# Raising the variances of every norm to the power -0.5 on GpSimd, in a hybrid decoder stack kernel

## The reference, cut to what matters

```python
def layer_norm(x, g, b):                # 3 per layer of the first stack, 6 in all
    mu = mean(x); var = mean(square(x - mu))
    return (x - mu) * rsqrt(var + 1e-5) * g + b
def rms_norm(x, g):                     # latents of the attention; all norms of the second stack
    return x * rsqrt(mean(square(x)) + 1e-6) * g
...
for l in range(2):                      # first stack
    h = layer_norm(ALPHA * h + 0.5 * swiglu(h, up1, down1), ...)
    h = layer_norm(ALPHA * h + hybrid_mixer(h, ...), ...)
    h = layer_norm(ALPHA * h + 0.5 * swiglu(h, up2, down2), ...)
for l in range(2):                      # second stack
    h = h + token_mixing(rms_norm(h), ...)
    h = h + (swiglu_2 if l == 0 else moe_swiglu)(rms_norm(h), ...)
out = rms_norm(h)
```

## Time and profile before

| | |
|---|---|
| median of 3 runs | 2813.24 us (2811.03, 2813.24, 2813.75) |
| profiled execution, span from first to last instruction | 2809.8 us (no other time of this execution is given) |
| PE busy | 2745.6 us, 98% of the span |
| DVE busy | 1982.1 us, 71% |
| ACT busy | 1608.7 us, 57% |
| POOL busy | 700.7 us, 25% |
| HBM | 661.01 MB read, 236 GB/s over the span |

### The profile page before, as it was taken

One profiled execution on the slowest core, in us unless ns is written; L12 is line 12 of the kernel. 1 busy time (PEld: TensorE's weight loads), 2 busy tenths in 40 slices (PEclk: granted clock), 3 DMA queues, 4 the chain that ended last, 5 costly groups with the idle time before them and its releaser, 6 DMA issues.

```text
span 2809.8 us, 68032 instructions
## 1 busy us (share of the span) xinstructions
PE 2745.6 (98%) x28028; PEld 2292.6 (82%) x28028; DVE 1982.1 (71%) x1914; ACT 1608.7 (57%) x1723; POOL 700.7 (25%) x562
## 2 busy tenths in 40 slices
PE   9999999999999999999999999999999999999997
PEld 7887788888877888887888887888879788797794
DVE  5457575564576755666855566778899898998986
ACT  5445663354356554455643445657677776777765
POOL 4314022122122221120122011144234243242331
PEclk9999999999999999999999999999999999999999
DMA  9764367576643676553576663469999999999995
GB/s 240 171 199 124 91 194 195 169 191 176 188 134 106 180 206 178 157 181 121 179 189 180 200 187 124 151 240 365 383 386 383 387 387 378 394 383 382 388 384 223
DMA packets 657516, 665.64 MB, mean 237 GB/s; under 512 B 25302, under 2 KB 513116, under 8 KB 657276
## 3 DMA queue, kind: packets, MB, share of 16 engines
q1 hardware_dynamic: 655696, 659.75, 71.5%
q0 software_dynamic: 704, 0.59, 0.4%
q10 hardware_dynamic: 876, 1.79, 0.2%
HBM read 661.01 MB, written 1.05 MB: 236 GB/s over the span
## 4 chain that ended last, share of the span: by engine, by line
PE 91%; DVE 4%; ACT 2%; issue 1%; DVEq 1%; DMA 0%; POOLq 0%; ACTq 0%; SPq 0%; POOL 0%
PE ps L2084 23%; PE ps L2085 23%; PE ps L2086 23%; PE ps L2814 3%; PE ps L2813 3%; PE ps L2812 3%; PE ps L2127 1%; PE ps L2133 1%; PE ps L2128 1%; DVE w_lo L1258 1%; PE ps L2437 1%; PE ps L2417 1%; ACT w_hi L705 1%; PE ps L2747 1%; PE ps L2505 1%
## 5 line engine op out<-in xcount | busy, mean ns | idle before, releaser
L2084 PE MATMUL ps<-x_hi,w_hi 128*128 128x128 f16 (+2 forms) x5440 | 1229.5, 250 | 16.1 <-DVE prod L1273 5.4
L2085 PE MATMUL ps<-x_lo,w_hi 128*128 128x128 f16 (+2 forms) x5440 | 1229.2, 250 | 0.0
L2086 PE MATMUL ps<-x_hi,w_lo 128*128 128x128 f16 (+2 forms) x5440 | 1229.0, 250 | 0.0
L1258 DVE SCALAR_TENSOR_TENSOR w_lo<-w,w_hi 128x2048 f16<-128x2048 f32 (+4 forms) x338 | 692.5, 2059 | 309.4 <-ACT w_hi L705 307.6
L705 ACT ACTIVATE w_hi<-w 128x2048 f16<-128x2048 f32 (+4 forms) x338 | 560.9, 1669 | 83.7 <-PE ps L2086 70.4
L2084 PEld LDWEIGHTS ps<-x_hi,w_hi 128*128 128x128 f16 x5440 | 534.0, 98 | 71.2 <-issue 14.4
L2085 PEld LDWEIGHTS ps<-x_lo,w_hi 128*128 128x128 f16 x5440 | 533.8, 98 | 45.9
L2086 PEld LDWEIGHTS ps<-x_hi,w_lo 128*128 128x128 f16 x5440 | 533.9, 98 | 42.6
L1754 DVE SCALAR_TENSOR_TENSOR w_lo<-w,w_hi 128x2048 f16<-128x2048 f32 x224 | 532.8, 2406 | 40.9 <-ACT w_hi L1178 40.8
L1178 ACT ACTIVATE w_hi<-w 128x2048 f16<-128x2048 f32 x224 | 416.9, 1901 | 28.4 <-DMA w<-in_moe_w_gate 12.0
L2066 POOL CAST ff<-pb 128x512 f16<-128x512 f32 x56 | 137.6, 2458 | 568.5 <-DVE pb L1846 568.5
(11 more groups left out here) (390 smaller groups left out, 4302.3 us busy)
## 6 DMA issues: line engine op xcount, KB each, us to landing
w<-in_ffn_w_up SPq DMA_DIRECT2D x176, 512.0 KB, 5.0
w<-in_moe_w_gate SPq DMA_DIRECT2D x80, 1024.0 KB, 8.1
w<-in_moe_w_up SPq DMA_DIRECT2D x80, 1024.0 KB, 8.7
w<-in_moe_w_down SPq DMA_DIRECT2D x64, 1024.0 KB, 7.8
w<-in_w_in SPq DMA_DIRECT2D x112, 512.0 KB, 4.6
mix<-in_moe_w_down SPq DMA_DIRECT2D x48, 1024.0 KB, 8.0
w<-in_mix_w_in SPq DMA_DIRECT2D x64, 512.0 KB, 4.9
mix<-in_moe_w_gate SPq DMA_DIRECT2D x32, 1024.0 KB, 8.9
```

The costliest lines, as they stand in the source:

```text
L1258: vec.scalar_tensor_tensor(k.w_lo[:, s, 0:size], k.w32[:, s, 0:size], WS, k.w_hi[:, s, 0:size], ALU.mult, ALU.subtract).then_inc(k.parts_r ...
L2084: pe.matmul(acc, w_hi, x_hi, start=first, stop=False)
L2085: pe.matmul(acc, w_hi, x_lo, start=False, stop=False)
L2086: return pe.matmul(acc, w_lo, x_hi, start=False, stop=last)
```

## The change

All roots and reciprocals of norms go. One POOL instruction, a TENSOR_TENSOR with the power as its operation and a column of -0.5 broadcast over the tokens as second operand, takes the place of each pair. DVE brings the variance to SBUF and adds the epsilon there; for the latents and the heads that is a new operation on DVE or ACT. `root_ready` and its table loads go, and at the norms' place ACT's next weight split moves ahead of the last square. The last norm is done per half, so that the first half's scaling can start before the second half's squares are summed.

```diff
+    k.minus_half = sb("minus_half", [P, 1], F32)
...
 (ACT, down_norm; wo_norm, wout_squares and down_squares alike)
                 c = u // 2
                 if c == KC - 1:
-                    root_ready()
+                    split(phase.first + phase.units + AHEAD, quads, UNIT)
                 act.wait_ge(k.vec_evac, vec0 + phase.base + 2 + c + 1)
                 square(n, c)
...
 (ACT, layer_norm)
         act.activation(k.tmp[:, 1, t], k.ps[:, 4, t], ACT.Square).then_inc(k.rest_squared, 1)
-        act.wait_ge(k.ln_spread, n + 1)
-        act.activation(k.std[:, 0, t], k.tmp[:, 1, t], ACT.Sqrt, bias=k.eps[:, 0:1]).then_inc(k.ln_std, 1)
-        split(following + 2, q, UNIT)
...
 (ACT, latents)
-                act.activation(k.sq[:, 0:3, :], k.mix1[:, 12:15, :], ACT.Square).then_inc(k.lat_squared, 1)
-            if u == LAT_ROOT:
-                act.wait_ge(k.lat_mean, l + 1)
-                act.activation(k.std[:, 0, :], k.ps[:, 4, 0:T1], ACT.Sqrt, bias=k.eps[:, 1:2], scale=float(D) / 256)
-                act.activation(k.std[:, 1, :], k.ps[:, 5, 0:T1], ACT.Sqrt, bias=k.eps[:, 1:2], scale=float(D) / 128).then_inc(k.lat_std, 1)
+                act.activation(k.sq[:, 0:2, :], k.mix1[:, 12:14, :], ACT.Square, scale=(D / 256) ** 0.5)
+                act.activation(k.sq[:, 2, :], k.mix1[:, 14, :], ACT.Square, scale=(D / 128) ** 0.5).then_inc(k.lat_squared, 1)
...
 (ACT, take_mean of the mLSTM heads)
-                           ACT.Sqrt, bias=k.eps[:, 2:3], scale=4.0 * float(D) / P).then_inc(k.act_evac, 1)
+                           ACT.Identity, bias=k.eps[:, 2:3], scale=4.0 * float(D) / P).then_inc(k.act_evac, 1)
...
 (DVE, layer_norm)
-        vec.tensor_tensor(k.tmp[:, 1, cols], k.ps[:, 5, cols], k.tmp[:, 1, cols], ALU.subtract).then_inc(k.ln_spread, 1)
+        vec.scalar_tensor_tensor(k.tmp[:, 1, cols], k.ps[:, 5, cols], LN_EPS * WS * WS, k.tmp[:, 1, cols], ALU.add, ALU.subtract).then_inc(k.ln_var_out, 1)
         u(0)
-        vec.wait_ge(k.ln_std, n + 1)
-        vec.reciprocal(k.rstd[:, 0, cols], k.std[:, 0, cols])
         vec.drain()
+        vec.wait_ge(k.ln_rooted, n + 1)
...
 (DVE, rms_norm; the latents alike, over 544 columns)
-        vec.wait_ge(k.rms_std, n + 1)
-        vec.reciprocal(k.rstd[:, 0, 0:T2], k.tmp[:, 0, 0:T2])
-        vec.drain()
+        vec.wait_ge(k.rms_mean, n + 1)
+        vec.tensor_scalar(k.tmp[:, 0, 0:T2], k.ps[:, 5, 0:T2], RMS_EPS, None, ALU.add).then_inc(k.rms_var_out, 1)
+        vec.wait_ge(k.rms_rooted, n + 1)
...
 (DVE, end of the second stack's attention)
         split_gated(12)
-        invert_ml(0)
         split_gated(13)
-        invert_ml(1)
-        vec.drain()
+        vec.wait_ge(k.ml_rooted, 2 * l + 2)
...
 (POOL)
+    def root(out, x, shape):
+        return pool.tensor_tensor(out, x, k.minus_half[:, 0:1].broadcast_to(shape), ALU.pow)
+
+    def ln_root(n):
+        t = kept(n)
+        pool.wait_ge(k.ln_var_out, n + 1)
+        root(k.rstd[:, 0, t], k.tmp[:, 1, t], [P, t.stop - t.start]).then_inc(k.ln_rooted, 1)
...
         down_norm(l * 3)
+        ln_root(l * 3)
+        pool.wait_ge(k.lat_var_out, l + 1)
+        for c in range(2):
+            a = root(k.rstd[:, c, :], k.tmp[:, c, :], [P, T1])
+        a.then_inc(k.lat_rooted, 1)
...
+        for pair in range(2):
+            pool.wait_ge(k.act_evac, s["rest"].base + REST_OUT["mean%d" % pair] + 1 + 2)
+            for h in range(4 + 2 * pair, 6 + 2 * pair):
+                a = root(k.sq[:, h, 0:T2], k.sq[:, h, 0:T2], [P, T2])
+            a.then_inc(k.ml_rooted, 1)
```

More of the change, by code:

```diff
@@ L772, in wo_norm, with layer_norm @@
         square(n, 6)
+        split(phase.first + phase.units + AHEAD, q, UNIT)
         act.wait_ge(k.vec_evac, vec0 + phase.base + 2 + 4)
         square(n, 7)
-    def layer_norm(n, b0, q, following, last=False):
+    def layer_norm(n, b0, last=False):
         act.wait_ge(k.ln_rest, n + 1)
@@ L810, in wout_squares @@
             else:
+                if c == 7 and l == 0:
+                    split(phase.first + phase.units + AHEAD, 0, UNIT)
                 act.wait_ge(k.vec_evac, phase.base + 2 + c // 2 + 1)
@@ L822, in down_squares, with rms_norm @@
         over_units_ahead(act, phase, 0, split, take, loop=False)
[L824 to L830, removed]
+    def rms_norm(n, to_parts=True):
+        if to_parts:
             for c in range(KC):
@@ L892, in act_program @@
         down_norm(l * 3, S1["down1"], q, vec0, take_vectors)
-        layer_norm(l * 3, C1["ln_b"], q, S1["win"].first)
+        layer_norm(l * 3, C1["ln_b"])
         def take_columns(u, b):
@@ L1008, in act_program @@
         wo_norm(l * 3 + 1, l, q, vec0)
[L1009 removed]
+        layer_norm(l * 3 + 1, C1["ln_b"] + KC)
         up(S1["up2"], q, vec0, gates0 + S1["up2"].gates, live(l), b0=C1["ln_b"] + KC)
@@ L1242, in act_program @@
     for b in range(2):
-        act.activation(k.squares[:, b, :], y[:, b, :], ACT.Square, accum_out=k.ms[:, b, 0:1])
-    act.drain()
-    act.activation(k.ms[:, :, 1], k.ms[:, :, 0], ACT.Sqrt, bias=k.eps[:, 1:2], scale=1.0 / D).then_inc(k.final_std, 1)
+        act.activation(k.squares[:, b, :], y[:, b, :], ACT.Square, accum_out=k.ms[:, b, 0:1]).then_inc(k.final_squared, 1)
     for b in range(2):
@@ L1460, in towards_latents @@
             if u == LAT_NORMED:
-                vec.wait_ge(k.lat_std, l + 1)
-                vec.reciprocal(k.rstd[:, :, :], k.std[:, :, :])
-                vec.drain()
+                vec.wait_ge(k.lat_mean, l + 1)
+                vec.tensor_scalar(k.tmp[:, 0:2, :], k.ps[:, 4:6, 0:T1], RMS_EPS, None, ALU.add).then_inc(k.lat_var_out, 1)
+                vec.wait_ge(k.lat_rooted, l + 1)
                 for c in range(3):
@@ L1648, in fox_low @@
                               ALU.subtract).then_inc(k.fox_parts, 1)
-        def invert_ml(pair):
-            vec.wait_ge(k.act_evac, rest.base + REST_OUT["mean%d" % pair] + 1 + 2)
-            for h in range(2 * pair, 2 * pair + 2):
-                vec.reciprocal(k.sq[:, 4 + h, 0:T2], k.sq[:, 4 + h, 0:T2])
         split_gated(2)
@@ L1885, in vec_program @@
     vec.wait_ge(k.final_g_loaded, 16)
-    vec.wait_ge(k.final_std, 1)
-    vec.reciprocal(k.ms[:, :, 2], k.ms[:, :, 1])
-    vec.drain()
     y = k.ps[:, 4:8, :].rearrange("p (b c) n -> p b (c n)", b=2)
     for b in range(2):
+        vec.wait_ge(k.final_squared, b + 1)
+        vec.tensor_scalar(k.ms[:, b, 1:2], k.ms[:, b, 0:1], 1.0 / D, RMS_EPS, ALU.mult, ALU.add).then_inc(k.final_var_out, 1)
+        vec.wait_ge(k.final_rooted, b + 1)
         vec.scalar_tensor_tensor(k.out_rows[:, b, :], y[:, b, :], k.ms[:, b, 2:3], k.final_g, ALU.mult, ALU.mult).then_inc(k.row_ready, 1)
@@ L2077, in pool_program @@
         moe_round(1)
+    for b in range(2):
+        pool.wait_ge(k.final_var_out, b + 1)
+        root(k.ms[:, b, 2:3], k.ms[:, b, 1:2], [P, 1]).then_inc(k.final_rooted, 1)
 def pe_program(pe, k, i, out):
```

39 lines of the change are left out of this document (24 added, 15 removed).

## The result

The changed kernel takes **3690.98 us** (median of 4 runs, 3689.78 to 3692.18) against 2813.49 of the kernel before (4 runs, 2811.03 to 2813.78). The ratio is 1.3116, with a 95% interval of 1.3098 to 1.3135: slower by 31%, or 877 us. The sign of the prediction (slower, with a chance of 0.52) held. Its size (2850) and its range (to 2909) did not.

What follows compares the result with a forecast made beforehand. PE, busy 98% of the span, was taken as the bound, so only its pauses count. Norms, latents and heads less gains lose 27.9 us, the clock 8.5: 36.4 over 2813.2 gives 2850 us, range 2797 to 2909.

Steps and rivals of the forecast that it cites:

- What a power costs on POOL: Step bounding a 272-column power between 3.3 and 7.3 us, using DVE's reciprocal-to-add ratio of 4.3; middle taken, 4.8.
- X: Time of one power of 272 columns on POOL, taken as 4.8 us (4.5 for 256 columns).
- the case above 7.3: Rival of a long function or code fetched on each call: X of 7.3 us and more, 2909 us; chance 0.15.
- layer norms: At the six layer norms the power lengthens the chain from variance to first scaling: 14.5 us lost.
- RMS norms: At the four RMS norms the power lengthens the chain from ACT's root to the first scaling: 10.8 us lost.
- latents: DVE's queue waits behind POOL's powers, so the last low part reaches PE 3.2 us late: 6.4 lost for both layers.
- heads: Four powers a layer end 1.3 us late, within 2 us of slack: no cost; beyond, about 3.8 per microsecond of X.
- less 3.8: Gains in the sum: 2.8 us from table loads at the heads, 1.3 at the last norm, minus 0.3 for latents' squares.
- the clock: PE's longer pauses lower its clock at half of the ten norms: 8.5 us lost, bounds none and 17.
- ACT's loads: 20 table loads go; those ahead of the gate's tanh at the heads win 1.4 us a layer, 2.8 in all.
- the cheap rival: A power is about as cheap as an add (X = 0.77): 15.6 us won, 2797 us; chance 0.33 for X below 2.0.
- Code fetched anew: Part of the rival with X of 7.3 and more: POOL fetches the power's code each time; 2909 us, chance 0.15.

Runs made afterwards that it cites:

- e4: The kernel before, with powers of several shapes, exponents and types added at the end of POOL's program: 2946.5 us.
- e2: The changed kernel with constant products for the powers of latents, RMS norms and heads; the six layer norms and the last norm keep theirs: 3051.6 us.
- e8: The kernel before with per-half last norm, one root for all heads, and ACT's exp(-0.5 ln(x)) for root and reciprocal in the other norms: 2804.2 us.
- e9: The changed kernel with ACT's exp(-0.5 ln(x)) in place of every POOL power but the last norm's; the weight split stays moved: 2800.6 us.
- e1: The changed kernel with every power but the last norm's replaced on POOL by a product of two constants of the same shape: 2792.4 us.

## Why the prediction was wrong

**The step that failed** is "What a power costs on POOL". I bounded X by 7.3 us, DVE's ratio of a reciprocal to an add (4.3) put on POOL's multiply by a column operand. The ratio of a power to the plain multiply of the same form is 67 on POOL. X is 43.7, nine times my 4.8 and six times my upper bound. DVE's ratio said nothing of another engine's implementation, and as no row excluded a far longer function, the case above 7.3 (0.15) should have had no end at 2909. e4 shows a price that is a constant 159 ns for each column, with 0.3 us fixed. The Trainium skill pointed the right way: "GPSIMD Engine Reference", section 3.1, makes a longer body cost in proportion to its operations. I had set it aside for want of a row. No run here varies the number of operations, so the rule itself is not shown.

**What stood around X held in the main.** With the measured X my own formulas give: layer norms 4 x (43.7 - 2.33) + 2 x (41.1 - 2.2) = 243; RMS norms 39.2 + 3 x 39.3 = 157; latents 2 x (231.7 + 0.9 + 87.4 + 7.5 - 246.5) = 162; heads 2 x (1336.8 + 164.4 - 1353.5 - 2) = 291; less 3.8. That is 850 us. With 1.7 for the clock at each of 14 pauses (24) it is 874, against 877.5 measured.

- *Layer norms.* A longer chain is on the path in full: e2's waits are 245.8 where the formula's difference gives 252. A shorter one is so only with the weight split out of its way: e8 won 0.3 us of PE's 1.4, e9 all of it.
- *RMS norms.* PE waits 38.6 to 39.9 at each, as a chain of 41.1 less its cover.
- *Latents.* PE's wait is 83.0; the formula gives 81.0. DVE's queue behind the wait was the right reason. The term of 7.5 us for DVE's work was 9.8, as the convolution, which I took at nothing, met DVE's first `w_lo` there. The sum has no term for these 2.3 us.
- *Heads.* "little above X = 4.8 it is used up" was right as a rule: the wait is 146.0 and the formula gives 145.7. The 3.8 per microsecond of X had been worked out; only X was missing.
- *ACT's loads.* The 20 loads are gone (45 before, 25 now). The wait of 2.23 us was to shrink to about 0.8 whatever X is: 0.74 at 1807.92. So a load off PE's path gave back 1.5 us, not the whole wait.
- *The clock.* I took a fall at half of the norms, with 1.7 us lost at each. It fell to 0.50 in all 14 pauses, and PE's busy time grew by 35.5 us net, 2.5 a pause: the 850 and 35.5 make 886, 8 above the measured 877.5. So the 874 is as near as it is partly by luck: the clock cost more than 1.7 a pause, and the rest of the change gave back more than my terms have (e1 is 5 us under the cheap rival's 2797.6).
- *Break-even and the cheap rival.* The cheap rival's 2797 is nearly e1's 2792: at 0.64 us the change would have been a gain. The terms as they stand break even at X = 2.6, not 2.7.
- *Code fetched anew.* That rival is excluded here: 43.75 us for the first power, 43.71 for the mean. The 6 us that the Trainium skill ("GPSIMD Engine Reference", section 2.1) gives for the first call of a freshly loaded routine show in no run here.

## What to carry to other kernels

An operation that no row of the trace shows is the first thing to price, by itself, before the chain around it is counted: one power of 256 columns on GpSimd costs as much as 67 multiplies, and it costs by the column, so it is usable at one column (0.57 us) and ruinous at 256. A bound taken from another engine's ratio is no bound, and its upper end should stay open. A chain of small operations between two matmul phases is worth a microsecond per microsecond only as long as nothing else stands in the queue of the engine that hands over; shortening it (e8) and moving what stood behind it (e9) belong together.

## What the runs showed of the hardware

- GpSimd's power: 159 ns per column whatever the partitions (1, 32 or 128), exponent (-1, -0.5, 0.5, 2), type (f32, bf16) or value; 0.57 us for one column with DVE idle, 2.4 us for one that began inside a DVE split.
- Behind pauses of 39 to 43, 83 and 146 us PE began at a granted clock of 0.50 every time. It stayed there for 2.8 to 5.8 us behind twelve of 14, with no order by the pause's length (2.8 to 5.3 behind the four of 43 us, 5.8 and 5.4 behind 83, 4.2 and 4.1 behind 146), and for 12.1 and 10.6 us behind two, although PE was busy for 97% and 100% of these stretches.
- DVE's `w_lo` of 768 columns that met POOL's 1088-column product took 3.12 us in place of 0.96 and ended 0.81 us behind it. Two `w_lo` that began inside a power of 41 us took their usual 2.29 us.
- One table set for logarithm and exponential serves both with a single load of 1.28 us, and two activations of 272 columns in a row take 0.94 us from the first's start to the second's end (203.72 to 204.66 in e9), half of DVE's reciprocal of 1.85.
